# Two attentions of a Trainium2 kernel: cumulative sums as two single-pass products, softmax weights divided before they are turned, squares added ahead of one product, and the sides of values and output exchanged

## What is computed

```python
# dilated heads: 8 heads of 64; three patterns, (window, dilation) = (128, 1), (512, 4), (2048, 16)
w = dens * jnp.exp(maxes - jnp.max(maxes, axis=0, keepdims=True))
w = w / jnp.sum(w, axis=0, keepdims=True)
o_dil = jnp.sum(w[..., None] * outs, axis=0)
# stick-breaking heads: 8 heads of 64
log_beta = jax.nn.log_sigmoid(z)
log_keep = jnp.where(causal, jax.nn.log_sigmoid(-z), 0.0)
between = lax.cumsum(log_keep, axis=3, reverse=True) - log_keep
weights = jnp.where(causal, jnp.exp(log_beta + between), 0.0)
...
mixed = jnp.concatenate([_rmsnorm(o_dil, g_dil_out), _rmsnorm(o_sb, g_sb_out)], axis=-1)
x = x + gate_mix * (mixed @ w_out)
```

## Time and profile before

| what | value |
|---|---|
| median of 3 runs | 1103.03 us (1102.2 to 1103.37) |
| profiled execution: its own time | 1103.41 us |
| its span in the trace | 1101.6 us |
| busy: PE, DVE, ACT, POOL | 1013.5, 506.0, 385.4, 493.7 us |
| mean granted TensorE clock | 0.984 of full |
| attention stage | about 528 to 655 us |
| experts stage | about 665 to 1101 us |

### The profile page before, as it was taken

One profiled execution on the slowest core, in us unless ns is written; L12 is line 12 of the kernel. 1 busy time (PEld: TensorE's weight loads), 2 busy tenths in 40 slices (PEclk: granted clock), 3 DMA queues, 4 the chain that ended last, 5 costly groups with the idle time before them and its releaser, 6 DMA issues.

```text
span 1101.6 us, 17641 instructions
## 1 busy us (share of the span) xinstructions
PE 1013.5 (92%) x7438; PEld 742.1 (67%) x7438; DVE 506.0 (46%) x916; ACT 385.4 (35%) x549; POOL 493.7 (45%) x209
## 2 busy tenths in 40 slices
PE   7999999999999999999999999899898777878777
PEld 6989988788788888887999895344444333434332
DVE  1998887565368675123345643322332221212113
ACT  7345545654574453456595431000000000000002
POOL 6987799879498976987664410000000000000000
PEclk9999999999999999999999999999999999998899
DMA  9754455557379998738334879999999999999995
GB/s 382 274 173 172 153 191 194 188 200 274 131 266 396 355 383 332 267 115 338 126 130 147 330 319 420 415 427 426 426 426 425 426 427 426 426 426 426 425 424 210
DMA packets 38530, 342.01 MB, mean 310 GB/s; under 512 B 4274, under 2 KB 4658, under 8 KB 6323
## 3 DMA queue, kind: packets, MB, share of 16 engines
q1 hardware_dynamic: 37152, 337.56, 76.8%
q10 hardware_dynamic: 1298, 3.32, 0.8%
HBM read 339.81 MB, written 1.05 MB: 309 GB/s over the span
## 4 chain that ended last, share of the span: by engine, by line
PE 71%; DMA 20%; DVE 5%; ACT 1%; SPq 1%; issue 1%; POOL 0%; another core or an unknown queue 0%; DVEq 0%; ACTq 0%
DMA ring<-in_gu 17%; PE ps L531 16%; PE ps L533 16%; PE ps L532 16%; PE ps L1167 6%; PE ps L1214 6%; DMA ring<-in_dn 3%; PE ps L1203 3%; PE ps L1147 1%; SPq L2523 1%; PE ps L525 1%; PE ps L713 1%; DVE rd L2213 1%; PE ps L929 1%; DVE ar L2401 1%
## 5 line engine op out<-in xcount | busy, mean ns | idle before, releaser
L2467 POOL TENSOR_TENSOR spl<-raw,sph 128x1024 fp32r<-128x1024 f32 x204 | 493.3, 2452 | 147.2 <-ACT sph L1271 147.0
L1271 ACT ACTIVATE sph<-raw 128x1024 fp32r<-128x1024 f32 x204 | 208.3, 1057 | 109.8 <-PE ps L533 88.3
L2401 DVE TENSOR_TENSOR ar<-ar,ps 64x256 f32<-64x256 f32 x32 | 13.5, 423 | 260.1 <-ACT ar L1739 260.1
L1739 ACT ACTIVATE ar<-ps 64x256 f32<-64x256 f32 x32 | 12.1, 378 | 326.2 <-PE ps L1167 326.2
L1214 PE MATMUL ps<-ar,ar 128*128 128x512 f32 x256 | 120.3, 613 | 0.0
L531 PE MATMUL ps<-sph,xbh 128*128 128x512 f32 x304 | 119.9, 394 | 0.0
L533 PE MATMUL ps<-sph,xbl 128*128 128x512 f32 x304 | 118.5, 390 | 0.0
L532 PE MATMUL ps<-spl,xbh 128*128 128x512 f32 x304 | 118.4, 389 | 0.0
L531 PE MATMUL ps<-xah,sph 128*128 128x256 f32 x320 | 91.9, 287 | 0.9 <-DVE xal L1801 0.6
L1831 DVE SCALAR_TENSOR_TENSOR ps<-ar,COL,ps 128x256 f32<-128x256 f32 x232 | 92.1, 486 | 0.0
L532 PE MATMUL ps<-xal,sph 128*128 128x256 f32 x320 | 90.5, 283 | 0.0
(11 more groups left out here) (314 smaller groups left out, 1632.7 us busy)
## 6 DMA issues: line engine op xcount, KB each, us to landing
raw<-in_stream SPq DMA_DIRECT2D x127, 1024.0 KB, 6.3
ring<-in_gu SPq DMA_DIRECT2D x46, 2048.0 KB, 44.8
ring<-in_dn SPq DMA_DIRECT2D x22, 2048.0 KB, 45.1
ring<-in_gu SPq DMA_DIRECT2D x24, 1024.0 KB, 11.0
ring<-in_dn SPq DMA_DIRECT2D x14, 1024.0 KB, 9.5
ar<-in_gu SPq DMA_DIRECT2D x7, 1024.0 KB, 26.0
slotx<-in_gu SPq DMA_DIRECT2D x5, 1024.0 KB, 37.7
ar<-in_dn SPq DMA_DIRECT2D x3, 1024.0 KB, 46.8
```

The source lines that it names most:

```text
L1271: e.activation(u.half(SPH[u.n % NSP], h), u.half(RAW[u.slot], h), ACTF.Copy).then_inc(w.up(hi_ok), 1)
L1739: e.activation(HS[x % 2][0:64, :], ps[bank_of["gu", x]][0:64, 0:256], ACTF.Silu)\
L2401: e.tensor_tensor(h[0:64, :], h[0:64, :], ps[bank_of["gu", x]][64:128, 0:256], ALU.mult)\
L2467: e.tensor_tensor(u.half(SPLO[u.n % NSP], h), u.half(RAW[u.slot], h), u.half(SPH[u.n % NSP], h), ALU.subtract).then_inc(w.up(lo_ok), 1)
```

## The change

Seven edits, all in attention and around it:

1. `sb_sums`: the 128 x 1536 logarithms are split like weights: ACT copies a high part (`logs`, new `sb_high`; in group 0 also a rounded copy `ou` of the ones and the triangular matrix), DVE subtracts a low part (`lbl`, new `sb_low`). TensorE then does, for each of four heads, a 384-column and a 128-column single-pass matmul on each part, in place of four 128-column fp32 ones.
2. Dilated weights are multiplied by `count`, summed and divided while queries are still the partitions: new `di_norm` on DVE, for each group eight multiplications with `accum_out` (128 and 256 columns by turns), one reciprocal of 128 x 8, and eight multiplications by a per-partition scalar. `di_turn` now waits for these; ACT copies the turned weights out of PSUM (`di_turned`). The matmuls of the row sums and DVE's L2205, L2213 and L2215 are gone.
3. `o_sum`: DVE first adds the four blocks of squares to one (new `o_add`, 128 x 512 and 128 x 256); TensorE does one 256-column fp32 matmul in place of four.
4. Order: vs before vd, stick-breaking values and norm before the dilated ones. In the output, k = 4 to 7 of W0, W1 and W2 come first, then k = 0 to 3 of each.
5. A small product `cb` and its copy come earlier.
6. `spread_gate(0)` moves from before `o_sum` to the first expert.
7. SP: the expert DMAs n = 4 to 12 go out in another order, each with its own wait; from n = 13 on the list is as before.

The diff, cut to its core:

```diff
-    put("count", np.concatenate([count[:, o:o + 128].T for o in (0, 128, 256)], 1))
+    put("count", count)
...
-        ISSUED = [0, 1, 2, 4, 5, 6, 3] + list(range(7, len(EXPERT_WEIGHTS)))
+        ISSUED = [0, 1, 2, 4, 8, 12, 5, 6, 9, 10, 11, 3, 7] + list(range(13, len(EXPERT_WEIGHTS)))
...
-                    e.matmul(ps[b][:, 0:128], upto, LB[g][:, h, 0:128], start=True, stop=True)
-                    e.matmul(ps[b][:, 128:256], upto, LB[g][:, h, 128:256], start=True, stop=False)
-                    e.matmul(ps[b][:, 128:256], ones, LB[g][:, h, 256:384], start=False, stop=True)
-                    e.matmul(ps[b][:, 256:384], upto, LB[g][:, h, 256:384], start=True, stop=True)\
-                        .then_inc(w.up(sbs_mm), 1)
+                    for i, P in enumerate((LOGS, LBL[g])):
+                        e.matmul(ps[b][:, 0:384], upto_r, P[:, h, :], start=(i == 0), stop=False)
+                        mm = e.matmul(ps[b][:, 128:256], ones_r, P[:, h, 256:384], start=False, stop=(i == 1))
+                    mm.then_inc(w.up(sbs_mm), 1)
...
             def di_turn(g):
                 for h in range(4):
-                    w.wait_ge(die_ok, 8 * g + 2 * h + 2)
+                    w.wait_ge(od_ok, 17 * g + 2 * h + 11)
...
-            vv("vd", 0)
-            di_turn(0)
-            vv("vd", 1)
-            di_turn(1)
-            di_values(0)
-            di_values(1)
-            vv("vs", 0)
-            o_sum("d", 0)
-            vv("vs", 1)
-            sb_values(0)
-            sb_values(1)
-            spread_gate(0)
-            o_sum("s", 1)
-            out_part(0, (0, 1, 2, 3), True, False)
-            out_part(1, (0, 1, 2, 3), True, False)
-            out_part(0, (4, 5, 6, 7), False, True)
-            out_part(1, (4, 5, 6, 7), False, True)
-            out_part(2, range(8), True, True)
+            vv("vs", 0)
+            vv("vs", 1)
+            di_turn(0)
+            sb_values(0)
+            sb_values(1)
+            di_turn(1)
+            vv("vd", 0)
+            o_sum("s", 0)
+            vv("vd", 1)
+            di_values(0)
+            di_values(1)
+            out_part(0, (4, 5, 6, 7), True, False, (0,))
+            o_sum("d", 1)
+            out_part(0, (4, 5, 6, 7), True, False, (1,))
+            out_part(1, (4, 5, 6, 7), True, False)
+            out_part(2, (4, 5, 6, 7), True, False)
+            out_part(0, (0, 1, 2, 3), False, True)
+            out_part(1, (0, 1, 2, 3), False, True)
+            out_part(2, (0, 1, 2, 3), False, True)
...
+            def di_norm(g):
+
+                hg, c = 4 * g, c_("count")
+                halves = [(h, tt, o, m) for h in range(4) for tt, o, m in ((0, 0, 128), (1, 128, 256))]
+                for h, tt, o, m in halves:
+                    w.wait_ge(die_ok, 8 * g + 2 * h + tt + 1)
+                    own()
+                    e.scalar_tensor_tensor(out=LB[g][:, h, o:o + m], in0=LB[g][:, h, o:o + m], scalar=1.0, in1=c[:, o:o + m],
+                                           op0=ALU.mult, op1=ALU.mult, accum_out=mx3[:, tt, hg + h:hg + h + 1])\
+                        .then_inc(w.up(od_ok), 1)
+                invert(mx3[:, :, hg:hg + 4], od_ok)
+                for h, tt, o, m in halves:
+                    own()
+                    e.tensor_scalar(LB[g][:, h, o:o + m], LB[g][:, h, o:o + m], mx3[:, tt, hg + h:hg + h + 1], None, ALU.mult)\
+                        .then_inc(w.up(od_ok), 1)
+
+            def o_add(kind, n):
+
+                w.wait_ge(osq_ok, 3 * n + 2)
+                for m in (512, 256):
+                    own()
+                    e.tensor_tensor(OSQ[kind][:, 0:m], OSQ[kind][:, 0:m], OSQ[kind][:, m:2 * m], ALU.add)\
+                        .then_inc(w.up(ors_ok), 1)
...
-                elif n == 13:
+                elif s == 13:
                     raws_free(2)
-                elif n == 14:
+                elif s == 14:
                     raws_free(3)
```

More of the change, by code:

```diff
@@ L982, in o_sum @@
                 claim(b)
[L983 to L987, removed]
+                w.wait_ge(ors_ok, 7 * n + 2)
+                e.matmul(ps[b][:, 0:256], ones, OSQ[kind][:, 0:256], start=True, stop=True).then_inc(w.up(os_mm), 1)
+                free[b] = [(ors_ok, 7 * n + 3)]
             def spread_gate(j):
@@ L995, in spread_gate, with out_part @@
                 free[b] = [(mr_ok, j + 1)]
-            def out_part(n, ks, start, stop):
+            def out_part(n, ks, start, stop, halves=(0, 1)):
                 u = units[first["w_out_2"] + n]
                 H, L = k8(SPH[u.n % NSP]), k8(SPLO[u.n % NSP])
-                for h in range(2):
+                for h in halves:
                     if start:
@@ L1027, in tensor @@
             sb_scores(1)
+            b = bank("cb")
+            claim(b)
+            w.wait_ge(cw_ok, 2)
+            e.matmul(ps[b][:, 0:36], ones, CWS, start=True, stop=True).then_inc(w.up(cb_mm), 1)
+            free[b] = [(cw_ok, 4)]
             qk("kd0")
@@ L1228, in tensor @@
                     gate_up(x, (0, 1))
-                if x == 0:
-                    spread_gate(1)
                 if x == NE:
@@ L1236, in tensor @@
                     gate_up(x, (2, 3))
+                if x == 0:
+                    spread_gate(0)
+                    spread_gate(1)
                 if 1 <= x < NE:
@@ L1624, in sb_soft, with sb_high @@
                 e.activation(LB[g], LB[g], ACTF.Ln, bias=c_("one")).then_inc(w.up(sbe_ok), 1)
+            def sb_high(g):
+                w.wait_ge(*((sbs_mm, 4) if g else (sb_mm, 8)))
+                w.wait_ge(sbm_ok, 11 if g else 5)
+                if g == 0:
+                    o = const_at["ones"][0]
+                    assert const_at["upto"][0] == o + 128
+                    e.activation(OU, CST[:, o:o + 256], ACTF.Copy).then_inc(w.up(sbe_ok), 1)
+                e.activation(LOGS, LB[g], ACTF.Copy).then_inc(w.up(sbe_ok), 1)
             def sb_weights(g):
@@ L1671, in scalar @@
             take(first["kd0"])
+            sb_high(0)
             sb_soft(1)
@@ L1675, in scalar @@
             take(first["kd1"])
+            sb_high(1)
             sb_weights(0)
@@ L1678, in scalar, with di_turned @@
             di_soft(0)
-            take(first["vd"])
+            take(first["vs"])
             sb_weights(1)
             di_soft(1)
+            take(first["vs"] + 1)
+            def di_turned(g):
+                for h in range(4):
+                    w.wait_ge(dt_mm, 4 * g + h + 1)
+                    e.activation(LT[g][:, h, :], ps[bank_of["dt", g, h]][:, 0:384], ACTF.Copy).then_inc(w.up(lt_ok), 1)
+            vv("vs")
+            warm(ACTF.Sqrt)
+            di_turned(0)
+            take(first["vd"])
+            o_square("s", 0)
+            o_square("s", 1)
+            di_turned(1)
+            o_root("s", 0)
             take(first["vd"] + 1)
+            o_high("s", 0, 0)
+            o_high("s", 0, 1)
             vv("vd")
-            warm(ACTF.Sqrt)
-            take(first["vs"])
+            take(first["w_out_2"])
             o_square("d", 0)
             o_square("d", 1)
-            take(first["vs"] + 1)
-            o_root("d", 0)
-            o_high("d", 0, 0)
-            o_high("d", 0, 1)
-            vv("vs")
-            take(first["w_out_2"])
-            o_square("s", 0)
-            o_square("s", 1)
-            spread_gate(0)
-            o_root("s", 1)
-            o_high("s", 1, 0)
-            o_high("s", 1, 1)
+            o_root("d", 1)
+            o_high("d", 1, 0)
+            o_high("d", 1, 1)
             for n in range(1, 4):
@@ L2241, in vector @@
             sb_scores(1)
+            sb_low(0)
+            w.wait_ge(cb_mm, 1)
+            own()
+            e.tensor_copy(CB, ps[bank_of["cb"]][:, 0:36]).then_inc(w.up(cw_ok), 1)
+            own()
+            e.memset(RT[:, :, 36:42], -4.0 * BIG).then_inc(w.up(cw_ok), 1)
             sb_soft(1)
             sb_sums(0)
+            sb_low(1)
             di_scores(0)
@@ L2248, in vector @@
             di_max(1)
-            di_turn(0)
-            di_turn(1)
-            di_values(0)
-            di_values(1)
-            heads_norm("d", 0, "g_dil_out_2")
-            w.wait_ge(cb_mm, 1)
-            own()
-            e.tensor_copy(CB, ps[bank_of["cb"]][:, 0:36]).then_inc(w.up(cw_ok), 1)
-            own()
-            e.memset(RT[:, :, 36:42], -4.0 * BIG).then_inc(w.up(cw_ok), 1)
-            heads_norm("s", 1, "g_sb_out_2")
+            di_norm(0)
+            di_norm(1)
+            o_add("s", 0)
+            heads_norm("s", 0, "g_sb_out_2")
+            o_add("d", 1)
+            heads_norm("d", 1, "g_dil_out_2")
             for k in range(8):
```

82 lines of the change are left out of this document (37 added, 45 removed).

## The result

| | before | changed |
|---|---|---|
| median | 1103.2 us (1102.2 to 1104.46, 4 runs) | 1110.75 us (1110.29 to 1112.37, 4 runs) |
| span of the profiled run | 1101.6 us | 1109.0 us |

The ratio is 1.0072, with a 95% interval of 1.006 to 1.0084: the change makes the kernel 7.6 us slower, 1.2 us less than the forecast of 1112.0.

The account below looks back on a forecast made before the run. Expert DMAs at about 426 GB/s bound the end, which follows T; TensorE savings against VectorE's division and port waits gave +8.3, taken as +9.0: 1103.4 + 9.0 = 1112.4, as median 1112.0 us, range 1101 to 1118.

Parts of the forecast that it names:

- T: Output product's start of the part finishing W0; DMA n = 14 follows 8.0 us later; forecast 641.5 against 633.2 us.
- (a): GpSimd's split of vd0 holds up the first multiplication of group 0's division: 2 us lost.
- The undisturbed price: Division of dilated weights on VectorE without GpSimd beside it: 6.9 us a group, 6.1 to 7.9.
- rival of a halved rate: Accumulating costs VectorE one more cycle per element, 1.6 us a group: 1114.5 to 1117 us; within a 0.20 dearer case.
- (b): GpSimd's split of vd1 falls into group 0's division on VectorE: 4.2 us lost.
- (c): GpSimd's split of W0 falls into group 1's division on VectorE: 4.1 us lost.
- From E to T: From group 1's last turned head to the output part finishing W0: 26.3 us, plus 1.0 for a clock dip.
- late `sb_low(1)`: Group 1's logarithm subtraction just behind a GpSimd split: maxima end at 592.5, not 589.7; +10.4 instead of +8.3.
- costed at nothing: ScalarE's logarithm copies delaying exponentials by 0.9 us, small product and copy 0.5 us, `spread_gate` 1 us: taken as hidden.
- Not held up: Rival: division and addition of squares lose nothing to GpSimd's splits; -5.0 us, 1098; chance 0.17.
- Port kept: Rival: VectorE, once begun, holds GpSimd off; 1102 to 1103.5 us; chance 0.13 together with partly blocked.
- A split product at fp32's speed: Rival: the sums' split matmuls not single-pass in speed, 7.1 us a group, +3.5 on the first date: 1115 us.

Follow-up runs that it names:

- f4: Changed kernel with the splits of vd1, W0 and W2 later, vd0's product ahead of group 1's turning, and the norm's product after W0: 1101.79 us.
- h1: f4 with expert DMA entry 8 sent out behind entries 12, 5 and 6: 1098.77 us.
- g1: Kernel before with only the split single-pass sums, the earlier small product `cb` and `spread_gate(0)` at the first expert: 1102.45 us.
- e4: Changed kernel with the expert DMAs in the order of the kernel before: 1110.03 us.
- f3: Changed kernel with five unused matmuls ahead of each group's turning of dilated weights: 1110.07 us.
- f2: Changed kernel with ScalarE's split of W2 moved behind the squares of the dilated heads: 1108.79 us.
- f1: Kernel before with only the split logarithms and single-pass sums: 1100.9 us.

## Why the prediction was right

**What bounds the kernel: right, with a limit.** In the table, distance and time agree to within 1.1 us for all kernels but two: f4, whose last idle time is elsewhere (3.0 us slower than h1 at one distance), and g1, whose median lies 1.9 us above its distance. Inside the profiled runs the fit is closer: the last instruction ends 459.7 to 461.6 us behind the issue of n = 14 in every kernel (before 460.4, after 461.3, g1 461.4) but f4, with 462.8; the rest of g1's excess, beyond that 1.0, stays open. "The end moves with T, one for one" holds as long as the DMA engines run empty ahead of n = 14; in before and after they do, so the step held where it was used. That "the other order of n = 4 to 12 only fills an earlier gap" was right for the change (e4), and would have been wrong for f4.

**The sums: right.** 2.4 us a group forecast, 2.33 measured, 2.7 us of distance in all.

**When VectorE is ready: right in date, not in course.** The maxima were to end at 589.7, and they do (588.23 plus 1.46), in part by luck: measured from the first sum this is 1.7 us late. The scale of 128 x 8 numbers, 0.22 us in the earlier trace rows, took 1.46 because the split of vd0 (584.89 to 589.66) lay on it. The 2 us of item (a), which I had put on the first multiplication, came here as 1.3, and that multiplication ran at 0.29. So the loss of (a) was found one instruction earlier, and the two differences, 1.7 late and 2.0 not lost, cancel but for 0.3 us.

**The undisturbed price: right.** The eight multiplications take 3.7 us with their reads (589.79 to 593.46) against 3.9; the accumulator's read takes 0.08 us against 0.1; the scalar ones 2.81 against 2.8. The rival of a halved rate falls: 0.29 and 0.43 us are what the two-input rows gave without accumulation. The Trainium skill's "Vector Engine (DVE) Microarchitecture Reference", section "Points that are easy to get wrong", says otherwise of this form with two fp32 sources in SBUF; here the measurement decides.

**The disturbed price: right.** (b) 4.2 forecast, 4.05 measured (6.86 less 2.81). (c) 4.1 forecast, 3.9 measured (2.25 and 2.37 less 0.29 and 0.43). VectorE gets one instruction in between GpSimd's two halves; it never kept the port. What no row of before could show, a scalar multiplication with one SBUF tensor, is held up too: its longest is 2357 ns. The Trainium skill's "SBUF — State Buffer", section "SBUF: two separate sides", says this of the 2-port modes; by that rule, the trace agrees. Group 1's last head was to be turned at 614.2; it was at 612.4, which from the first sum is 614.1 in before's dates.

**From E to T: right.** I gave 26.3 us and 1.0 for the clock. T is 632.53 (first output matmul behind the norm's product) plus five half-parts of 1.44 (twelve matmuls each, for four blocks of one half of a unit; the 24 given above are for both halves), 639.7: 27.3 behind E. The clock's 1.0 is the 1.05 us of vd0 named at f3. The additions of squares ended 7.5 us behind vd1 against 7.3, and f2 shows their share beside the split of W2 to be 2.0.

**The size.** T +8.3 was the sum, and I took +9.0 to allow for a late `sb_low(1)`, which did not happen (1.80 us). That allowance is 0.7 of the 1.2 us by which 1112.0 lay too high; the rest is that the end moved 0.6 less than n = 14 did from the first sum, which is within the 1 us to which the two agree in other kernels. The range of 1101 to 1118 took in "no change" as well; what the result bears out is the sum and its own range of 1108.5 to 1115.5.

**What was wrong.** Some numbers beside the sum do not come out by its own terms. With the maxima at 592.5 the 2 us of (a) would not be lost, which makes the late `sb_low(1)` worth +0.8 and T +9.1, not +10.4; a free read and no dip give +5.7, not +5.5. Sums at fp32's speed would cost 7.1 us in both groups, and by the counting that gives 2.6 saved the time would be near 1121, not 1115. None of them enters the 1112.0 but through the +9.0. Of "8 us earlier" for TensorE alone, the 1.0 of `spread_gate` was not to be had (g1); the sum did not use it. And of the work "costed at nothing", `sb_high` and `sb_low` were covered as said, since f1 keeps the whole gain.

**Rivals.** Not held up: refuted for this order by the rows above. f4 and h1 show what it is worth when one split misses the division, one misses the addition and the third is covered; h1's -4.2 us is near the -5.0 given for no loss at all, but with other orders of products and DMAs. Port kept: refuted by the rows above. A split product at fp32's speed: refuted by 2.33 us a group.

## What to carry to other kernels

When work moves from instructions that read PSUM to ones that live in SBUF alone, look for what GpSimd does at that moment: here each of its 2.35 us instructions beside the division cost what was left of it, and three splits cost VectorE 10 us (4.05, 3.9 and 2.0) at places where TensorE waited for it. The remedy need not be less work: an in-order engine given other products ahead of the wait, or a split issued some microseconds later, gave 4 us each. And where transfers bound the end, find the last moment at which they run dry, again after each edit, for it moves.

## Of the hardware, not expected

A VectorE instruction of 128 x 8 elements with one SBUF input waited for GpSimd (1.46 us against 0.17 for the same instruction in the other group, with GpSimd idle); the reduction just ahead of it, beside the same split and with one SBUF input too, took 1.22 us for 1024 elements, as it did in before (0.69 for 512), and did not wait. So one SBUF input alone does not decide it. Reading VectorE's accumulator costs 75 to 84 ns and delays the next instruction by about as much (128-column multiplications of 0.29 us start 0.41 before the next one, where gaps are otherwise 0.03). TensorE's clock fell to 1.2 GHz behind a wait of 2.0 us that followed 3.5 us of full work (f3), and did not fall in 597 to 604 us where the matmuls filled the wait.
